# A hybrid decoder trunk on one core: the first norm's modulation by TensorE in packed, turned blocks, and a new order of modulation units in the first FFN

## What is computed

```python
cond = silu(c)                                   # c: one vector of 1024
for l in range(2):
    mod = cond @ ada_w[l] + ada_b[l]             # 1024 x 9216 weights a layer
    sh0, sc0, gt0, sh1, sc1, gt1, sh2, sc2, gt2 = split(mod, 9)
    h = rms_norm(x, g[l, 0]) * (1 + sc0) + sh0   # x: 256 tokens x 1024
    x = x + 0.5 * (1 + gt0) * swiglu(h, ffn_w_in[l, 0], ffn_w_out[l, 0])    # 1024 -> 2 x 2816 -> 1024
    h = rms_norm(x, g[l, 1]) * (1 + sc1) + sh1
    x = x + (1 + gt1) * token_mixer(h, ...)      # RWKV-7 and mLSTM branches
    h = rms_norm(x, g[l, 2]) * (1 + sc2) + sh2
    x = x + 0.5 * (1 + gt2) * swiglu(h, ffn_w_in[l, 1], ffn_w_out[l, 1])
return rms_norm(x, final_g)
```

## Time and profile before

| | |
|---|---|
| runs | 1403.44, 1404.10, 1399.76 us; median 1403.44 |
| profiled execution | 1401.57 us, span from first to last instruction 1399.8 us |
| TensorE busy | 1380.5 us, 99% of the span |
| VectorE busy | 1035.5 us, 74% |
| ScalarE, GpSimd busy | 299.8 us (21%), 68.4 us (5%) |
| read from HBM | 280.10 MB, 201 GB/s over the span |

### The profile page before, as it was taken

How to read it: one execution, slowest core, us unless ns; L and a number is a source line. 1 busy time by engine, 2 the same in 40 slices (tenths; PEclk the granted TensorE clock), 3 DMA queues, 4 the chain that set the end, 5 groups by cost and what they waited for, 6 DMA issues and landing times.

```text
span 1399.8 us, 30879 instructions
## 1 busy us (share of the span) xinstructions
PE 1380.5 (99%) x13632; PEld 1304.0 (93%) x13632; DVE 1035.5 (74%) x1738; ACT 299.8 (21%) x580; POOL 68.4 (5%) x137
## 2 busy tenths in 40 slices
PE   7999999999999999999999999999999999999998
PEld 3999999889988999999999999988898889999998
DVE  5899889778723769987888886887883365856565
ACT  3111101452322031110031110034432302211101
POOL 5010000000000000100000000000000000000000
PEclk9999999999999999999999999999999999999999
DMA  9999785443433758887767886544434257456530
GB/s 347 329 339 324 284 313 174 140 141 104 115 75 122 240 183 276 280 298 292 244 217 248 274 283 241 174 126 143 146 96 105 72 198 241 154 184 205 202 129 31
DMA packets 218085, 283.14 MB, mean 202 GB/s; under 512 B 15272, under 2 KB 183584, under 8 KB 217952
## 3 DMA queue, kind: packets, MB, share of 16 engines
q1 hardware_dynamic: 199008, 211.12, 47.1%
q0 software_dynamic: 17952, 69.21, 14.0%
q10 hardware_dynamic: 992, 0.85, 0.2%
HBM read 280.10 MB, written 1.05 MB: 201 GB/s over the span
## 4 chain that ended last, share of the span: by engine, by line
PE 97%; SPq 1%; DMA 1%; issue 0%; DVE 0%; ACT 0%; ACTq 0%; DVEq 0%
PE ps L1870 96%; DMA arena<-in_ada_w_dram 1%; PE ps L1874 1%; SPq L559 0%; SPq L554 0%; PE ps L2367 0%; DVE hT L1855 0%; DVE x L1257 0%; ACT xn L718 0%; ACTq L254 0%; SPq L552 0%; SPq L551 0%; DVEq L1854 0%; ACTq L1060 0%
## 5 line engine op out<-in xcount | busy, mean ns | idle before, releaser
L1870 PE MATMUL ps<-hT,ring 128*128 128x128 f32 (+2 forms) x2384 | 373.4, 313 | 1.3 <-ACT hT L718 1.3
L1870 PEld LDWEIGHTS ps<-hT,ring 128*128 128x128 f32 (+1 forms) x2384 | 333.7, 191 | 32.3 <-issue 8.3
L1870 PE MATMUL ps<-y_both,arena 128*128 128x128 f32 x2304 | 266.6, 275 | 1.0 <-issue 1.0
L1870 PEld LDWEIGHTS ps<-y_both,arena 128*128 128x128 f32 x2304 | 261.8, 192 | 1.5 <-issue 1.5
L1870 PE MATMUL ps<-arena 32*32 32x32 f32 (+6 forms) x4368 | 203.5, 230 | 3.0 <-issue 3.0
L1870 PEld LDWEIGHTS ps<-arena 32*32 32x32 f32 (+3 forms) x4368 | 192.6, 138 | 12.1 <-issue 10.6
L1870 PE MATMUL ps<-arena,ring 128*128 128x128 f32 (+1 forms) x1344 | 190.8, 294 | 0.0
L1870 PEld LDWEIGHTS ps<-arena,ring 128*128 128x128 f32 x1344 | 175.2, 192 | 6.6
L1084 DVE SCALAR_TENSOR_TENSOR ada_acc<-ada_stage,cond,ada_acc 128x1024 f32<-128x1024 f32 (+1 forms) x119 | 149.0, 1252 | 5.5 <-DMA ada_stage<-in_ada_w_dram 1.5
L1870 PE MATMUL ps<-y_both,ring 128*128 128x128 f32 (+1 forms) x1024 | 150.8, 301 | 0.0
L1870 PEld LDWEIGHTS ps<-y_both,ring 128*128 128x128 f32 x1024 | 138.7, 192 | 6.5
(11 more groups left out here) (316 smaller groups left out, 1389.5 us busy)
## 6 DMA issues: line engine op xcount, KB each, us to landing
ring<-in_ffn_w_in_dram SPq DMA_DIRECT2D x86, 1024.0 KB, 7.7
ada_stage<-in_ada_w_dram POOLq DMA_DIRECT2D x66, 1024.0 KB, 5.9
ring<-in_ffn_w_out_dram SPq DMA_DIRECT2D x44, 1024.0 KB, 6.8
ring<-in_mix_w_in_dram SPq DMA_DIRECT2D x128, 128.0 KB, 2.3
ring<-in_mix_w_in_dram SPq DMA_DIRECT2D x12, 1024.0 KB, 6.0
ring<-in_mix_w_in_dram SPq DMA_DIRECT2D x6, 1536.0 KB, 6.5
ring<-in_mix_w_out_dram SPq DMA_DIRECT2D x8, 1024.0 KB, 5.0
ring<-in_mix_w_in_dram SPq DMA_DIRECT2D x14, 512.0 KB, 6.6
```

Source lines behind the costliest of these rows:

```text
L1870: return nc.tensor.matmul(out_, lhsT, rhs, start=start, stop=stop, **kw)
```

## The change

- The first norm: all four blocks by TensorE. `cond_wide` holds each column of cond as the first of 32 columns, the others zero. `rows_of` makes, for a tile of four parts of 128 rows, four products with such a stationary operand, part j into partitions 32j to 32j + 31 of a bank; the second tile of the block is added to it. So a bank holds four partial rows, in partitions 0, 32, 64 and 96. VectorE or ScalarE copies the whole bank, `rows_turned` turns it (four turns of 128 x 128), and VectorE adds the four parts by two small reductions at the head of `half_factors`.
- Block 0 and block 2 come first, then the first half column, block 1, the second half column, block 3. VectorE's `ada_sums` of the start go.
- `unread`: two, and later three, products of 256 columns whose result nobody reads, while the factors are made.
- `FIRST_PLACES` takes the place of `ADA_PLACES` in the first FFN of layer 0.
- The counts of `ada_done` start from zero; GpSimd's first two refills wait for TensorE instead of VectorE.

```diff
+FIRST_PLACES = [("up", s, 2 if 1 < s < STEPS - 5 or s == STEPS - 4 else 1) for s in range(1, STEPS - 2)] + \
+    [("down", p, 1) for p in range(7)] + [("down", 7, 2)]
...
-    n, total = UNITS * len(ada_blocks(l, half)), sum(w for _, _, w in ADA_PLACES)
+    places = FIRST_PLACES if l == half == 0 else ADA_PLACES
+    n, total = UNITS * len(ada_blocks(l, half)), sum(w for _, _, w in places)
...
+        cond_wide = sb("cond_wide", [P, KT, 32])
+        first_cols = sb("first_cols", [P, 16])
...
+        ada_rows = view(xn[:, :, :].rearrange("p a b -> p (a b)"), 4, BLOCK)
...
-                            po.wait_ge(ada_done, 4 * (v + 1) if v < 2 else 16 + 2 * (v - 1))
+                            if v < 2:
+                                po.wait_ge(*PE.at(None, f"first rows {v}"))
+                            else:
+                                po.wait_ge(ada_done, 2 * (v - 1))
...
+            ac.wait_ge(*DV.at(None, "cond room"))
+            act(cond_wide[:, :, 0], ps[:, 4, 0:8], ACT.Silu, "cond wide")
...
-                ac.wait_ge(*PE.at(None, f"row {n}"))
-                act(xn[0:1, n, 0:BLOCK], ps[0:1, n, :], ACT.Copy, f"row {n}")
+                ac.wait_ge(*PE.at(None, f"rows {2 + n}"))
+                act(ada_rows[:, 2 + n, :], ps[:, 1 - n, :], ACT.Copy, f"rows {2 + n}")
...
+                for row, bank in ((n, 3), (2 + n, 2 - n)):
+                    free(V.tensor_reduce(first_cols[:, 4 * row:4 * row + 4], quad(bank)[:, :, 0:P:32], AXX, ALU.add))
+                dv.wait_ge(*DV.last())
...
+            free(V.memset(cond_wide[:, :, :], 0.0), "cond room")
+            dv.wait_ge(*PE.at(None, "first rows 1"))
+            free(V.tensor_copy(ada_rows[:, 0, :], ps[:, 0, :]), "rows 0")
...
+            dv.wait_ge(*PE.at(None, "rows 1"))
+            free(V.tensor_copy(ada_rows[:, 1, :], ps[:, 2, :]), "rows 1")
...
+            def rows_of(bank, half, stage):
+
+                for j in range(4):
+                    last = mm(ps[32 * j:32 * j + 32, bank, :], cond_wide[:, 4 * half + j, :], stage[:, j, :],
+                              start=(half == 0), stop=(half == 1))
                 return last
...
+            def rows_turned(n, bank):
                 for i in range(4):
+                    last = turn(quad(bank)[:, i, :], ada_rows[:, n, i * P:i * P + P])
                 return last
+
+            def unread(n):
+
+                for i in range(n):
+                    mm(ps[:, 0, 0:T], ones[:, 0:P], ones[:, 0:T])
...
+            pe.wait_ge(*AC.at(None, "cond wide"))
             pe.wait_ge(*AC.at(None, "x 1 1"))
-            ada_row(0, 0, KT).then_inc(*PE.step("row 0"))
+            for u in range(2):
+                pe.wait_ge(ada_full[u], 16)
+                last = rows_of(0, u, ada_stage[:, u])
+                last.then_inc(*PE.step(f"first rows {u}"))
+            for u in range(2):
+                pe.wait_ge(first_full[2 + u], 16)
+                last = rows_of(1, u, ada_first[:, 2 + u])
+            last.then_inc(*PE.step("rows 2"))
             pe.wait_ge(params_full, 16 * 2)
             params("params next", 7, rest=False)
-            pe.wait_ge(*DV.at(None, "ada 0"))
-            ada_columns(3, 0, 0, 1, "ada 0")
-            row_columns(0, 8).then_inc(*PE.step("half"))
+            pe.wait_ge(*DV.at(None, "rows 0"))
+            rows_turned(0, 3)
+            pe.wait_ge(*AC.at(None, "rows 2"))
+            rows_turned(2, 2).then_inc(*PE.step("half"))
+            unread(2)
             pe.wait_ge(half_full, 32)
             first_halves(0)
-            ada_row(1, 0, ROW_TILES).then_inc(*PE.step("row 1"))
-            first_halves(1, (0,))
-            pe.wait_ge(*DV.at(None, "ada 1"))
-            ada_columns(3, 4, 1, 1, "ada 1")
-            row_columns(1, 12)
-            pe.wait_ge(*DV.at(None, "ada 3"))
-            ada_columns(3, 12, 3, 1, "ada", start=False)
-            first_halves(1, (1,))
+            pe.wait_ge(*DV.at(None, "factors 0"))
+            for u in range(2):
+                pe.wait_ge(first_full[u], 16)
+                last = rows_of(2, u, ada_first[:, u])
+            last.then_inc(*PE.step("rows 1"))
+            first_halves(1)
+            for u in range(2):
+                pe.wait_ge(first_full[4 + u], 16)
+                last = rows_of(0, u, ada_first[:, 4 + u])
+            last.then_inc(*PE.step("rows 3"))
+            pe.wait_ge(*DV.at(None, "rows 1"))
+            rows_turned(1, 3)
+            pe.wait_ge(*AC.at(None, "rows 3"))
+            rows_turned(3, 1).then_inc(*PE.step("ada"))
+            unread(3)
```

More of the change, by code:

```diff
@@ L1100, in ada_at @@
                         dv.wait_ge(*DV.last(l))
-                    ada_sums(wide, wide_stage(v), 0, 2, 2 * (n % UNITS), 16 + 2 * v)
+                    ada_sums(wide, wide_stage(v), 0, 2, 2 * (n % UNITS), 2 * v)
                     if n % UNITS == UNITS - 1:
                         for h in range(2):
-                            ins = ada_turned(ada_acc[:, h, :], 2 * (n // UNITS) + h, 16 + 2 * v + 2, None)
+                            ins = ada_turned(ada_acc[:, h, :], 2 * (n // UNITS) + h, 2 * v + 2, None)
                             link(l, ins, f"ada {half} {n // UNITS}" if h else None)
@@ L1396, in first_normed @@
                                      ALU.mult), f"normed start {2 * b + 1}")
-            dv.wait_ge(*AC.at(None, "cond"))
-            for u, stage, full in ((0, ada_stage[:, 0], ada_full[0]), (1, ada_stage[:, 1], ada_full[1]),
-                                   (2, ada_first[:, 0], first_full[0]), (3, ada_first[:, 1], first_full[1])):
-                acc = ada_acc[:, u // 2, :]
-                dv.wait_ge(full, 16)
-                ada_sums(acc, stage, 0, 4, 4 * (u % 2), 4 * u)
-                if u % 2:
-                    free(ada_turned(acc, u // 2, 4 * u + 4, None), f"ada {u // 2}")
-                if u == 1:
-                    dv.wait_ge(*AC.at(None, "rs start"))
-                    for k in range(2):
-                        free(V.tensor_tensor(hT[:, k, :], x[:, k, :], rs[:, :], ALU.mult), f"normed start {k}")
-                    first_normed(1)
-                    params(None, "params next", 7)
-                    dv.wait_ge(*PE.at(None, "half"))
-                    half_factors(0)
-                    first_tiles((3,))
-                    for b in (2, 3):
-                        first_normed(b)
@@ L1417, in _ @@
-            dv.wait_ge(first_full[5], 16)
-            for k in range(ROW_TILES, KT):
-                tile = ada_first[:, 5, k - 4, :]
-                if k == ROW_TILES:
-                    link(None, V.tensor_scalar(ada_acc[:, 0, :], tile, cond[:, k:k + 1], None, ALU.mult))
-                else:
-                    link(None, V.scalar_tensor_tensor(ada_acc[:, 0, :], tile, cond[:, k:k + 1], ada_acc[:, 0, :],
-                                                      ALU.mult, ALU.add))
-            link(None, V.transpose(ada_turn[:, :], ada_acc[:, 0, :]))
@@ L1426, in _ @@
-            free(V.tensor_reduce(ada_red[:, 3, :], view(ada_turn[:, :], 16, 32), AXX, ALU.add), "ada 3")
+            free(V.memset(cond_wide[:, :, :], 0.0), "cond room")
+            dv.wait_ge(*PE.at(None, "first rows 1"))
+            free(V.tensor_copy(ada_rows[:, 0, :], ps[:, 0, :]), "rows 0")
+            dv.wait_ge(*AC.at(None, "rs start"))
+            for k in range(2):
+                free(V.tensor_tensor(hT[:, k, :], x[:, k, :], rs[:, :], ALU.mult), f"normed start {k}")
+            first_normed(1)
@@ L1427, in _ @@
+            params(None, "params next", 7)
+            dv.wait_ge(*PE.at(None, "half"))
+            half_factors(0)
+            first_tiles((3,))
+            for b in (2, 3):
+                first_normed(b)
+            dv.wait_ge(*PE.at(None, "rows 1"))
+            free(V.tensor_copy(ada_rows[:, 1, :], ps[:, 2, :]), "rows 1")
             link(None, V.memset(stat[:, :, :], 0.0))
@@ L2055, in _ @@
             first_squares()
-            def ada_row(n, first, end):
-                for k in range(first, end):
-                    at = 2 * n + 2 + k // 4
-                    if k % 4 == 0:
-                        pe.wait_ge(first_full[at], 16)
-                    last = mm(ps[0:1, n, :], cond[:, k:k + 1], ada_first[:, at, k % 4, :], start=(k == 0),
-                              stop=(k == end - 1 and end != 4))
-                return last
-            def row_columns(n, at):
-                pe.wait_ge(*AC.at(None, f"row {n}"))
+            def rows_of(bank, half, stage):
+                for j in range(4):
+                    last = mm(ps[32 * j:32 * j + 32, bank, :], cond_wide[:, 4 * half + j, :], stage[:, j, :],
+                              start=(half == 0), stop=(half == 1))
+                return last
+            def rows_turned(n, bank):
                 for i in range(4):
-                    last = mm(ps[:, 3, at + i:at + i + 1], xn[0:1, n, i * P:i * P + P], ident[0:1, 0:1],
-                              start=(i == 0), skip_group_check=True)
```

(6 more changed lines are left out.)

7 lines of the change are left out of this document (3 added, 4 removed).

## The result

The change makes this kernel slower by about a quarter of a per cent. Of 17 runs each, the changed kernel has a median of 1405.2 us (1403.39 to 1407.3) and the kernel before 1401.83 us (1399.5 to 1404.1): ratio **1.0025** (95% interval 1.0017 to 1.0032), +3.4 us. Measured a second time beside other versions, the ratio was 1.0024 (1.0015 to 1.0033). The forecast was +6.2 us, by a start that loses 2.4 us and an end of the first FFN that loses 3.8. Both terms were wrong, the first in its sign: the start gained, and the end lost more than forecast. The profiled execution took 1406.26 us, its span is 1404.4 us (before: 1401.57 and 1399.8).

A forecast was written before the change was run, and what follows sets the result against it. TensorE was taken to bound the kernel; +2.4 us at the start and +3.8 at the first FFN's end gave +6.2: 1407.8 on the profiled execution, 1409.6 on the median. Own range 1406.5 to 1412, whole range 1399.5 to 1414.5.

The forecast's parts named there:

- What bounds the kernel: Whole run: TensorE's chain, 97% of the span; a change shortens it only where TensorE is not yet fed.
- Behind it TensorE always has work: After the first full tile product at 39.3 us, TensorE was taken never to lack work.
- Term one: The start, up to the first full product: 41.7 against 39.3 us, +2.4 us (bounds -4.1 and +16.4).
- I take two at a time: 4 batches of 0.88 = 3.5 us a block: Start: of four packed column groups only two run at once, so each row block costs TensorE 3.5 us.
- Rival A: Start: all four column groups run at once, 1.75 us a block, -4.1 there, 1403.1 in all; chance 0.22.
- TensorE did not wait there, so: nothing: Up part of first FFN: VectorE loses a 2.6 us unit and 2.9 us of turns; no effect on time.
- Term two: End of first FFN: unit 23 and its load come late, TensorE waits, +3.8 us (bounds +2.5 and +5.0).
- Rival D: Clock falls after the wait at 230 us: 2 to 6 us of slower products, 1412 to 1416; chance 0.08.
- two things by which it was to be found wrong: A block under 3 us at the start, or no TensorE gap at 230 to 235 us.

The follow-up runs named there:

- version 1: The changed kernel's new start alone, with the old order of units: 1402.52 us, ratio 1.0006 to the kernel before.
- version 8: Changed kernel with last unit one step later, sums seven products later, and all block parts in one column group (no packing): 1422.96 us, ratio 1.0152.
- version 2: The kernel before with the new order of units alone, keeping the old start: 1409.2 us, ratio 1.0053.
- version 4: The changed kernel with eight unread products of 256 columns ahead of the wait for the rows: 1402.92 us, ratio 1.0010.
- version 3: The changed kernel with the pair of units in down step 1 instead of 7: 1402.0 us, ratio 0.9999.
- version 12: version 3 with VectorE's last weight sums ahead of its last turns, and TensorE's modulation sums one product later: 1402.05 us, ratio 1.0001.
- version 7: Changed kernel with last unit one step later, sums seven products later, and no unread products in the start: 1404.05 us, ratio 1.0017.

## Why the prediction was wrong
- **What bounds the kernel** held at the two places that the prediction looked at. "Behind it TensorE always has work" was true only for a TensorE as late as that of the kernel before. It was read from a chain in which VectorE did not appear; the chain does not tell how far VectorE is from appearing. The timeline of the kernel before does: at the end of the up part ScalarE, which stands between the two, waits 2.67 us for TensorE and no more. In version 1's profile TensorE is 1.2 us earlier and VectorE 5.9 us later, and TensorE waits 2.7 us.
- **Term one failed** at the step "I take two at a time: 4 batches of 0.88 = 3.5 us a block". Measured are 1.74 to 1.86 us a block and 7.0 without packing. Rival A had it, and version 8 shows that packing is the cause. The evidence behind the choice was the spacing of instructions with 48 and 32 columns, 0.07 and 0.05 us for a batch of four, where one instruction alone would take 0.041 and 0.027. That is 0.03 and 0.02 us more, and at 512 columns a batch of four takes 0.46 us (1.85 / 4), 0.02 more than one instruction's 0.44. So all three fit one instruction plus 0.02 to 0.03 us a batch; the forecast took this addition for a factor of 1.7 to 1.9. What the addition is no run shows. The row of the 64 x 64 tiles, which spoke for rival A, was the nearer one. In sign and size this step gives +2.4 predicted against -2.2 to -3.1 measured. Rival A's -4.1 was too good by two things: "half" came at 22.1 where it had 19.8 (a slow sum of squares in that profile; with a fast one it is 20.1 to 20.4), and block 3's second tile lands only at 32.4 to 33.1 where TensorE waits for it. The Trainium skill, "TensorEngine Tiling (Array Packing)", section Theoretical Speedup, promises up to 4x for 32 columns; the measured 7.03 to 1.85 us is 3.8x and agrees. The Trainium skill's page "TensorE: Matmul & The Clock Gate", Part 3, gives 2.38x for three column tiles; no run here has three, and four gave 3.8x.
- **"TensorE did not wait there, so: nothing"** (the unit taken out of the last up step) failed. Version 1 against the changed kernel shows it: without that relief TensorE waits 2.7 us at 167.7 and another 1.3 at the end, and the start's gain is used up. None of the twelve profiles with the new order of units has this wait. What the relief alone is worth in the time was not measured.
- **Term two** had the right mechanism and place: one unit more behind down step 3, with unit 23's load issued only after unit 21. Its size was +3.8 with bounds of 2.5 and 5.0. The waits are 5.2 us in the changed kernel and 5.35 in version 2. I had let the load land early since the queues empty from 225 on the earlier trace rows; it took 7.88 us, the upper bound's value. Before it, unit 22 waited 1.64 us as well, which stood in no term.
- **Rival D came true in addition.** It had a chance of 0.08 and a cost of 2 to 6 us. The granted clock was 0.50 for some 6 us behind the wait; it cost 2.9 us by the timeline, 2.5 by version 4. A bound on a wait of 4 to 5 us should have included it as a term.
- **The sum:** -2.2 to -3.1 at the start, +5.2 for the waits, +2.9 for the clock, and -0.2 for the wait that stood there before, is +4.8 to +5.7. Measured are +3.4 by the medians and +4.6 by the profiles. So 1.4 to 2.3 us are not accounted for at the medians' level, about what the profiles with the new start get back behind the first FFN. The forecast of +6.2 came near this sum by two errors of opposite sign, which is luck. It was also added to a median of three runs, 1403.44; over 17 runs the kernel before has 1401.83.
- **The range** of 1399.5 to 1414.5 held the measured time. Of the two things by which it was to be found wrong, one happened: a block takes under 3 us.

## What to carry to other kernels
An engine that is off the path because it keeps up by a few us is off the path only as long as nobody gets faster and none of its loads is late: before a gain is counted, follow it to the end of the stage and ask which engine it will meet there. When small instructions stand for large ones, take the row nearest in length, and test whether the difference at the shortest is a factor or an addition before scaling it up. And price waits of TensorE like these (5.2 us in the changed kernel, 3.1 in versions 3 and 12, each in two pieces) with the half clock that can follow, 2.6 to 2.9 us here; filling them with unread products gives that part back, though the wait itself only yields to an earlier producer. Whether it follows can differ between executions of one kernel, so look at the clocks of all runs and not of the one profile.

## What was unexpected in the hardware
- Products with 32 stationary columns and 512 moving ones, four column groups, run truly at once in 32-bit float: 16 instructions in 1.85 us, where one group takes 7.03.
- TensorE waited 3.8 and 1.3 us with only nine short instructions between, and ran at half clock from about 234 to 241 us. The same wait filled with unread products left the clock at 1.00. In their profiles shorter waits cost the clock for as long: 1.8 + 1.3 us (version 3) and 0.7 + 2.4 us (version 12), both at half clock from about 231.3 to 238. In version 7 a single wait of 1.61 us, behind eight turns, was followed by 0.50 from 37 to 40 us, while a wait of 2.74 us between full products (version 1, before 167.72) left the clock at 1.00.
- The sum of squares at 11 us takes 3.72 or up to 5.9 us in different executions of the same code, with the granted clock given as 1.00 both times. There the profile's clock does not explain the pace.
- A load of 1 MB took 7.9 us (changed kernel, from 219.48) and 11.9 us (version 1, from 148.11) from issue to landing, while the queues together moved 330 to 425 GB/s for most of that time, against the median of 7.7 in the earlier trace rows. A chain of "unit done, next load, next unit" with two buffers therefore has no slack of its own once two units come in one step.
